# Chunk-mixer biases written four heads at a time into four PSUM banks, and the chunk products placed one head behind u

## What is computed

```
s = jnp.einsum('hij,bcjhd->bcihd', ws, vp) + jnp.transpose(b_s[:, :L])[None, None, :, :, None]
...
b_out = chunk_mix(u, vn, w_s, b_s) * jax.nn.silu(b_gate)     # u * s, four heads of 128 channels
y = x + jnp.einsum('bte,ed->btd', jnp.concatenate([a_out, b_out], axis=-1), w_out)
```

## Time and profile before

| what | us |
|---|---|
| median of 3 runs (lowest, highest) | 505.31 (504.54, 506.3) |
| the profiled execution: its own time | 504.52 |
| span of its slowest core, core 2 (all: 498.2 to 503.0) | 503.0 |
| PE busy | 468.0 (93%) |
| DVE busy | 338.6 (67%) |
| ACT busy | 175.6 (35%) |
| POOL busy | 101.7 (20%) |

### The profile page before, as it was taken

One profiled execution on the slowest core, in us unless ns is written; L12 is line 12 of the kernel. 1 busy time (PEld: TensorE's weight loads), 2 busy tenths in 40 slices (PEclk: granted clock), 3 DMA queues, 4 the chain that ended last, 5 costly groups with the idle time before them and its releaser, 6 DMA issues.

```text
span 503.0 us, 7722 instructions; the slowest of 8 cores (498.2 to 503.0 us)
## 1 busy us (share of the span) xinstructions
PE 468.0 (93%) x2416; PEld 214.0 (43%) x2416; DVE 338.6 (67%) x664; ACT 175.6 (35%) x293; POOL 101.7 (20%) x140
## 2 busy tenths in 40 slices
PE   0778999999999899999999999999999999999991
PEld 0433444444444344444444445444454445444440
DVE  1977537769767566876687757566664767886555
ACT  3124142490026402239133640023700380333044
POOL 8341011410051100251016100034000500161000
PEclk9989999999999899999999999999999999999996
DMA  7999999980059100540036000000000000220013
GB/s 192 157 155 161 204 194 203 159 122 1 1 116 147 32 1 1 196 140 2 2 115 221 3 5 1 0 3 26 4 1 0 1 1 1 85 106 2 1 42 125
DMA packets 23143, 36.85 MB, mean 73 GB/s; under 512 B 2688, under 2 KB 17152, under 8 KB 23072
## 3 DMA queue, kind: packets, MB, share of 16 engines
q0 software_dynamic: 15680, 14.94, 21.7%
q1 hardware_dynamic: 6704, 20.26, 13.2%
q10 hardware_dynamic: 720, 1.16, 0.6%
HBM read 42.06 MB, written 10.09 MB: 104 GB/s over the span
## 4 chain that ended last, share of the span: by engine, by line
PE 78%; DVE 8%; issue 5%; ACT 5%; POOL 2%; DMA 1%; ACTq 0%; DVEq 0%; another core or an unknown queue 0%; POOLq 0%
PE pF L490 50%; PE pF L942 19%; PE pT L474 3%; PE pF L926 2%; PE pF L923 2%; PE pF L704 1%; PE pF L894 1%; DMA xg<-x 1%; ACT vscr L742 1%; POOL Tt L531 1%; DVE vn_sb L573 1%; DVE xg L948 1%; DVE ss L557 1%; ACT vscr L449 1%; DVE mix L914 1%
## 5 line engine op out<-in xcount | busy, mean ns | idle before, releaser
L490 PE MATMUL pF<-hT,win 128*128 128x512 bf16 x1024 | 233.8, 382 | 3.9 <-DVE vn_sb L573 2.7
L490 PEld LDWEIGHTS pF<-hT,win 128*128 128x128 bf16 x1024 | 98.9, 98 | 121.3 <-issue 8.9
L942 PE MATMUL pF<-wout,mix 128*128 128x512 bf16 x512 | 114.7, 379 | 2.1 <-DVE wout L385 0.9
L942 PEld LDWEIGHTS pF<-wout,mix 128*128 128x128 bf16 x512 | 48.9, 98 | 58.2 <-issue 4.0
L563 POOL TENSOR_TENSOR ss<-ss,nhalf 128x4 f32<-128x4 f32 (+1 forms) x34 | 37.1, 1092 | 154.1 <-DVE ss L561 153.9
L490 PE MATMUL pF<-win,hT 128*128 128x512 bf16 x272 | 61.4, 384 | 0.0
L948 DVE TENSOR_TENSOR xg<-pF,xg 128x512 f32<-128x512 f32 x64 | 44.0, 688 | 21.5 <-PE pF L942 19.7
L449 ACT ACTIVATE vscr<-xg 128x1024 bf16<-128x1024 f32 x40 | 42.3, 1057 | 44.3 <-DVE xg L948 38.5
L464 ACT ACTIVATE hb<-xg,ssx 128x1024 bf16<-128x1024 f32 x28 | 32.0, 1144 | 67.0 <-PE pT L474 56.4
L554 ACT ACTIVATE vscr<-pF 128x512 f32<-128x512 f32 x32 | 19.1, 597 | 98.3 <-PE pF L490 67.2
L458 POOL TENSOR_TENSOR ssx<-ssx,nhalf 128x1 f32<-128x1 f32 (+1 forms) x22 | 15.0, 680 | 184.8 <-DVE ssx L456 166.8
(11 more groups left out here) (94 smaller groups left out, 335.2 us busy)
## 6 DMA issues: line engine op xcount, KB each, us to landing
xg<-x SPq DMA_DIRECT2D x16, 512.0 KB, 5.8
win<-w_in POOLq DMA_DIRECT2D x8, 1024.0 KB, 75.4
y<-xg SPq DMA_DIRECT2D x12, 512.0 KB, 2.9
wout<-w_out POOLq DMA_DIRECT2D x4, 1024.0 KB, 35.5
win<-w_in POOLq DMA_DIRECT2D x4, 256.0 KB, 18.2
win<-w_in POOLq DMA_DIRECT2D x2, 512.0 KB, 23.0
y<-hT SPq DMA_DIRECT2D x4, 256.0 KB, 2.2
y<-hT ACTq DMA_DIRECT2D x4, 256.0 KB, 2.5
```

The costliest lines, as they stand in the source:

```text
L490: r = h.matmul(out=out_ap, lhsT=lhsT(k), rhs=rhs(k), start=(k == 0), stop=(k == 7))
L942: r = h.matmul(out=pf[:, :], lhsT=mix[:, k, i * 128:(i + 1) * 128], rhs=wout[l][:, k, hf * 512:(hf + 1) * 512], start=(k == 0), stop=(k == 7))
```

## The change

The biases of the four heads go to partitions 0 to 1, 32 to 33, 64 to 65 and 96 to 97 of one tile. Four bias matmuls, one from each partition group, are issued together into four banks after u of head 0. `pool_mm(3)` follows, and then, for each head, u of the next head and the chunk product of this one. `s_pool` moves to a place right after u of head 0. The bias tables come as a (128, 258) transfer in place of a (2, 1024) one, and `prep_bias` works on 128 partitions by 256 columns. The identity gets a transfer of its own, ahead of the now smaller `cpk` on the same queue, into a staging area.

```
-            for g in range(4):
-                hh = g
+            def u_mm(hh):
                 pf, pfb = proj_fm(l, C_U + hh * 128)
-                if g == 0:
-                    pool_mm(3)
-                pf, pfb = bankF.alloc()
-                def f(h, pf=pf, hh=hh):
-                    h.matmul(out=pf[:, 0:GT].rearrange("p (c i) -> p c i", c=TPG), lhsT=ones2[:, :],
-                             rhs=bias2[:, l, hh, :].unsqueeze(1).broadcast_to([2, TPG, 128]), start=True, stop=False)
...
+            def bias_mm(banks):
+                def f(h):
+                    r = None
+                    for hh in range(4):
+                        q = slice(32 * hh, 32 * hh + 2)
+                        r = h.matmul(out=banks[hh][0][:, 0:GT].rearrange("p (c i) -> p c i", c=TPG), lhsT=ones[q, :],
+                                     rhs=bias2[q, l, :].unsqueeze(1).broadcast_to([2, TPG, 128]), start=True, stop=False)
+                    return r
+                S.emit(PE, f, reads=[buf("bias2"), buf("ones")], writes=[b for _, b in banks])
...
+            def chunk_mm(hh, pf, pfb):
...
+                     for c in range(TPG):
+                         r = h.matmul(out=pf[:, c * 128:(c + 1) * 128], lhsT=vn_sb[:, c, hh * 128:(hh + 1) * 128],
+                                      rhs=wsT[:, l, hh, :], start=False, stop=(c == TPG - 1))
...
+            u_mm(0)
+            at("u0")
+            banks = [bankF.alloc() for _ in range(4)]
+            bias_mm(banks)
+            pool_mm(3)
+            for hh in range(4):
+                if hh < 3:
+                    u_mm(hh + 1)
+                chunk_mm(hh, *banks[hh])
                 at(f"h{hh}")
...
-                hk["h0"] = [lambda: s_pool(l)]
+                hk["u0"] = [lambda: s_pool(l)]
...
-        ldma(bsf, bc(bs_d.rearrange("l h i -> (l h i)").rearrange("(o n) -> o n", o=1), 2), buf("bsf"))
+        ldma(g_bc[:, 0:258], bsr_d[:, :], buf("bsf"))
...
+        stage_ops.append(S.emit(ACT, lambda h: h.dma_start(out=identf, in_=cid_d[:, :]), writes=[buf("identf")], dma="cid"))
```

More of the change, by code:

```diff
@@ L215, in build_program @@
         epsb = sb("epsb", [128, 1], F32)
-        ones2 = sb("ones2", [2, 128], BF16)
+        ones = sb("ones", [128, 128], BF16)
+        bias2 = sb("bias2", [128, 2, 128], BF16)
         ssx = sb("ssx", [128, 96], F32)
@@ L250, in build_program @@
         yt = hT[:, :, :].rearrange("p k t -> p (k t)").bitcast(F32).rearrange("p (a d) -> p a d", a=2)
[L251 to L254, removed]
+        bsf = g_bc[:, 0:256]
+        m01 = g_bc[:, 256:258]
+        bhif = Tt[:, 0, 0:256]
+        bhi = hb[:, 1, 0:256]
+        blo = hb[:, 2, 0:256]
         pT = [ps(f"pT{i}", [128, D], BF16) for i in range(2)]
@@ L356, in build_program @@
         S.emit(DVE, lambda h: h.memset(epsb[:, :], EPS), writes=[buf("epsb")])
-        S.emit(DVE, lambda h: h.tensor_copy(out=ident[:, :], in_=identf), reads=[buf("identf")], writes=[buf("ident")])
-        S.emit(DVE, lambda h: h.memset(ones2[:, :], 1.0), writes=[buf("ones2")])
+        stage_ops.append(S.emit(DVE, lambda h: h.tensor_copy(out=ident[:, :], in_=identf), reads=[buf("identf")],
+                                writes=[buf("ident")]))
+        S.emit(DVE, lambda h: h.memset(ones[:, :], 1.0), writes=[buf("ones")])
         S.emit(DVE, lambda h: h.memset(ss4[:, :, :], 0.0), writes=[buf("ss4")])
@@ L376, in prep_bias @@
             S.emit(DVE, lambda h: h.tensor_scalar(out=bhif, in0=bhi, scalar1=m01[:, 0:1], scalar2=None, op0=ALU.mult),
[L377 to L380, removed]
+                   reads=[buf("bhi"), bb, buf("blo")], writes=[buf("bhif")])
+            S.emit(DVE, lambda h: h.scalar_tensor_tensor(out=bias2[:, :, :].rearrange("p l i -> p (l i)"), in0=blo,
+                                                         scalar=m01[:, 1:2], in1=bhif, op0=ALU.mult, op1=ALU.add),
+                   reads=[buf("blo"), buf("bhif"), bb], writes=[buf("bias2")])
         def state_sum(l, g):
@@ L910, in run_item, with f @@
             at("bg")
-            for g in range(4):
-                hh = g
+            def u_mm(hh):
                 pf, pfb = proj_fm(l, C_U + hh * 128)
-                S.emit(DVE, lambda h, pf=pf, hh=hh: h.tensor_tensor(out=mix[:, 4 + hh, :], in0=pf[:, 0:GT],
-                                                                    in1=mix[:, 4 + hh, :], op=ALU.mult),
+                S.emit(DVE, lambda h: h.tensor_tensor(out=mix[:, 4 + hh, :], in0=pf[:, 0:GT], in1=mix[:, 4 + hh, :],
+                                                      op=ALU.mult),
                        reads=[pfb, buf(f"mix{4 + hh}")], writes=[buf(f"mix{4 + hh}")])
-                if g == 0:
-                    pool_mm(3)
-                pf, pfb = bankF.alloc()
-                def f(h, pf=pf, hh=hh):
+            def bias_mm(banks):
+                def f(h):
                     r = None
-                    h.matmul(out=pf[:, 0:GT].rearrange("p (c i) -> p c i", c=TPG), lhsT=ones2[:, :],
-                             rhs=bias2[:, l, hh, :].unsqueeze(1).broadcast_to([2, TPG, 128]), start=True, stop=False)
+                    for hh in range(4):
[5 more added lines that the diff above has]
+            def chunk_mm(hh, pf, pfb):
+                def f(h):
+                    r = None
                     for c in range(TPG):
@@ L928, in f @@
                     return r
[L929 to L932, removed]
+                S.emit(PE, f, reads=[buf(f"vn{c}") for c in range(TPG)] + [buf(f"wsT{l}")], writes=[pfb])
+                S.emit(DVE, lambda h: h.tensor_tensor(out=mix[:, 4 + hh, :], in0=pf[:, 0:GT], in1=mix[:, 4 + hh, :],
+                                                      op=ALU.mult),
                        reads=[pfb, buf(f"mix{4 + hh}")], writes=[buf(f"mix{4 + hh}")])
+            u_mm(0)
[7 more added lines that the diff above has]
+                chunk_mm(hh, *banks[hh])
                 at(f"h{hh}")
@@ L1058 @@
     ident, inv, m01, mask = _consts()
+    shared["c_ident"] = ident
     shared["cpk_h"] = np.ascontiguousarray(np.concatenate(
-        [ident, shared.pop("norm_g").reshape(2, 8, 128).transpose(2, 0, 1).reshape(128, 16),
-         shared["pool_scale"].reshape(2, 4, 128).transpose(2, 0, 1).reshape(128, 8), inv, m01], axis=1))
+        [shared.pop("norm_g").reshape(2, 8, 128).transpose(2, 0, 1).reshape(128, 16),
+         shared["pool_scale"].reshape(2, 4, 128).transpose(2, 0, 1).reshape(128, 8), inv], axis=1))
+    bsr = np.zeros((4, 32, 258), dtype=np.float32)
+    bsr[:, 0:2, 0:256] = shared["b_s"].transpose(1, 0, 2).reshape(4, 1, 256)
+    bsr[:, :, 256:258] = m01
+    shared["bsr_h"] = bsr.reshape(128, 258)
     w_s = shared.pop("w_s")
     shared["wsk_h"] = np.ascontiguousarray(np.concatenate([mask, w_s.transpose(3, 0, 1, 2).reshape(128, 1024)], axis=1))
-    shared["wb_h"] = np.ascontiguousarray(np.concatenate([w_s[:, :, 0, 0].reshape(1, 8), shared["b_s"][:, :, 0].reshape(1, 8)],
+    shared["wb_h"] = np.ascontiguousarray(np.concatenate([w_s[:, :, 0, 0].reshape(1, 8), shared.pop("b_s")[:, :, 0].reshape(1, 8)],
                                                          axis=1))
```

23 lines of the change are left out of this document (11 added, 12 removed).

## The result

| | before | after |
|---|---|---|
| median of 5 runs (lowest, highest), us | 505.58 (504.54, 506.3) | 532.72 (529.57, 585.81) |
| ratio of the times | 1 | 1.0519 [1.0487, 1.0551] |
| the profiled execution, us | 504.52 | 533.65 |
| its span, slowest core (all), us | 503.0 (498.2 to 503.0) | 532.1 (527.1 to 532.1) |
| PE busy on that core | 468.0 (93%) | 465.3 (87%) |

The run of 585.81 us was a disturbed one and is left out of the ratio. The change makes the kernel slower by 0.0519 x 505.6 = 26.2 us. The forecast was +22.0 us, 527, in a range of 521 to 536.

The account below looks back on a forecast made before the run. PE's work and waits were taken to set the time (78% of the span is PE work). Head loops +22.8, start -0.2, output weights of item 0 -0.6 gave +22.0 us, 527, range 521 to 536.

Parts of the forecast that it names:

- The circle of banks: Head loop: u of heads 2 and 3 wait for banks of chunk products; 3.52 us between u runs, against 2.37.
- The packed biases: Head loop: four biases cost PE 0.41 us (low end) to 1.64; 1.23 us an item saved, lost waiting for u0's bank.
- Item by item: Head loops of all eight items: 8.6 + 6.6 + 2.4 + 5.2 = +22.8 us.
- The start: Before item 0: smaller `prep_bias` gains 0.2 us; the bias table may come up to 2.8 us later at no cost.
- The credit of 0.6 us in item 0: Item 0: PE's 0.64 us wait for output weights goes, as it arrives 3.3 us later; -0.6 us.
- (a): PE's new stands in the head loops lower its clock, one low stretch an item: +13 us, 540; chance 0.13.
- (b): Head loop: banks do not bind and the packing pays, 1.23 us an item saved: 495; chance 0.04.
- (c): Four biases don't pack but run one after another: up to 5.4 us more, 532; chance 0.10.
- (d): Waits and savings cancel to within 0.3%, needing two of three bank waits absent; chance 0.02.

Follow-up runs that it names:

- b1: Changed kernel, same order and packing, but u of heads 2 and 3 get other banks, read long before: 1.0034 of the kernel before, median 506.53 us.
- b8: Kernel before with each chunk product, its single bias and own bank, one head behind u; nothing packed, start untouched: 0.9986.
- b3: Changed kernel with chunk products of heads 0 and 1 right after the biases, then u and the next head's chunk product alternating: 0.9908; repeated, 0.9881.
- b7: b3 with all four bias matmuls reading partitions 0 to 1, one partition group: 0.9953 of the kernel before.
- b4: Kernel before with only the changed start and bias tile; single biases per head as before, from each head's partition group: 1.0037, +1.9 us.
- b6: b3 with the bias table as four transfers of two rows (8 KB) on a zeroed tile, in place of 129 KB: 0.9851.
- b9: b4 with the bias table as four transfers of two rows (8 KB) on a zeroed tile: 1.0004 of the kernel before.
- b10: Changed kernel with the bias table as four transfers of two rows (8 KB) on a zeroed tile: 1.0476 of the kernel before.
- b12: b6 measured again, on another occasion: 0.9869 of the kernel before.
- b5: b4 with eight tiny DVE memsets more at the head of DVE's list: 1.0036 of the kernel before.

## Why the prediction was right, and where it was off

**The circle of banks** was right in mechanism and in size. Forecast 3.52 us from u to u and from u3 to the output projection, 2.91 from u0 to u1; measured 3.49, 3.50, 3.50, and 2.91. The releaser is DVE's multiplication of the chunk product just computed, 16 times. b1 shows that it is the banks, b8 that it isn't the order, b3 that the packing isn't at fault either.

**The packed biases** cost 0.33 us for four, the low end that the forecast took, and b7 shows that this needs the four groups. As forecast, none of it is seen in the time, because u1 waits for u0's bank.

**Item by item**: items 2 to 6 14.3 for 13.8 (the sample rows of items 2 and 4 took 0.4 us more each), item 7 3.3 for 3.3, item 0's head loop 3.2 for 3.3. For all loops and what follows from them, the ratio of after less that of b4 gives 0.0482, 24.4 us, against 22.8 - 0.6 = 22.2. Item 1's step also holds item 2's wait and the clock. Core 2 of before had the low stretch of the earlier trace rows as core 1 of after has one, so that cancels; less the 0.4 us by which item 2's wait grew, 2.7 - 0.4 = 2.3 is left, for 2.4.

**The start** is the term that was mis-sized: "the transfer may be up to 2.8 us later at no cost". The sum asked when the table would be there for `prep_bias`, and it was in time or nearly so. It didn't ask what the new transfers do to the rest of the start. -0.2 was forecast, +1.9 measured (b4). Gate weights of item 0 come late where they never did before, the step from item 0 to 1 is 0.37 us longer, item 2's wait 0.4. The 121 KB more in the table carry a part, 1.8 us by the slowest core and 1.2 by the mean core; what carries the rest stays open.

**The credit of 0.6 us in item 0**: the wait for output weights went, as said, but there was nothing to gain by it. The kernel before shows it: its step from item 0 to 1 is 56.11 us on every core, with 0 to 1.59 us of that wait, since the transposes wait for DVE behind it. After their wait of 2.27 us the clock fell on five of eight cores, which cost 1.68 us on each (before, on none). The forecast was 4 us short: 2.1 for the start, and some 2.2 (24.4 - 22.2, with an uncertainty of nearly 2) for the rest, of which the credit and the clock are the parts that the traces show.

**Rivals.** (a) is wrong where it was placed: the granted clock stayed at 1.00 through the loops, with two stands of 1.39 us and one more in each. The Trainium skill's rule ("TensorE: Matmul & The Clock Gate", "A second HAM failure mode: psum-queue depth-cycling") isn't borne out in these loops, for stands of this length and number. At other places the clock did fall: on core 1 after waits of 2.3 to 3.5 us, and after item 2's wait of some 2.4 us on six of eight cores, against one before. With the five falls behind the transposes of item 0 that is ten more than before at these two places, an estimated 10 x 1.65 / 8 = 2.1 us on a core. So the mechanism of (a) did cost something, outside the loops and in part by the new start (five of eight in b4).

The prediction weighed (a) by one wait of before and found seven cores of eight against it. It overlooked another place in the same trace. At the start of item 0 a projection waits for the DVE reader of its bank (`vn_sb` L573), and the clock fell behind that on seven of eight cores, after 1.78 to 2.66 us. The timeline of core 1 before, and a window of it:

```profile
31.02 1.02 PE L490 MATMUL pF<-hT,win 128*128 128x512 bf16 x4 [1.79 <-DVE vn_sb L573]
33.02 3.21 PE L490 MATMUL pF<-hT,win 128*128 128x512 bf16 x8 [0.98 <-DVE vn_sb L573]
...
32.40:35.70 3.30, 2.68 (x7) 1.02 (x8) 3.07 (x11) 0.00 (x0) 1.65 (x3) 0.50 1.14 143
```

Waits of 1.79 us and, 2 us later, 0.98 us are not far from the forecast stands, so the chance of 0.13 rested on less than it seemed.

(b) holds for the packing, not for this order: b3 and b6 are that kernel, and took 497.9 us (b6) for its 495, with 1.1 us saved an item in place of 1.23, what item 0 gives back, and the start. (c) is out by 0.33 us. (d) didn't happen.

**Open.** Why the clock falls after the same wait on some cores and not on others, how the table costs its 1 to 2 us, and what makes the gate weights late, isn't settled by these runs. Undoing the identity's transfer of its own was not tried.

## What to carry to other kernels

Before results are spread over more buffers at once, write down the circle: for each hand-out, who reads the buffer's last contents, and where that reader's own input stands in the list. If it stands directly in front of the operation that wants the buffer, the two engines take turns, and no idle share of either will show it beforehand. A wait that goes is worth nothing if another one, for a later event, stands right behind it: look at several cores, where the first wait differs and the step doesn't. A saving on the busiest engine in front of a point where a transfer lands is given back there. And a new start wants a run of its own: here it was forecast at -0.2 us and cost 1.9.

## What was not expected of the hardware

- DVE stood 0.46 us between two operations of one line with nothing to wait for, on every core, at L534 in most kernels with the new start. One instruction more ahead of it moved it to an earlier operation (b6, b9, b10, b12), eight more took it out of that stretch (b5). The kernel before has such a stand too, on all eight cores, in item 4:

```profile
288.06 1.06 DVE L645 SCALAR_TENSOR_TENSOR smpb<-smp,vnf 16x128 bf16<-16x128 f32 x3 [0.47 <-DVE smpb L645]
```

  Counted through DVE's recorded list, semaphore operations included, the instruction behind such a stand of 0.45 to 0.48 us (after item 0) is always the 316th, 444th, 828th, 956th, 1084th or 1212th, in every kernel that has one and on every core, and these differ by multiples of 128. What is done there the runs don't show.
- PE's clock stayed at 1.00 through stands of 1.39 us, two within 7 us, and fell after waits of 1.8 to 3.5 us, but not on all cores: after item 2's wait of 2.0 to 2.4 us on one of eight cores before, six after, five in b4, three in b5 and two in b9, and after the wait of 1.8 to 2.7 us in item 0 on seven of eight before. The length of one wait alone does not decide it.
